# Expert layer one: two successive pairs of experts share one frame of output rows

## The reference, cut to what matters

```python
# layer one of the reference (hier_moe), one expert layer of a two-block decoder
g_prob = softmax(t @ w_group_router + b_group_router)            # 4 groups, the best one
g_w, g_idx = lax.top_k(g_prob, 1)
e_logits = (t @ w_expert_router + b_expert_router).reshape(-1, 4, 8)[group of the token]
e_prob = softmax(e_logits)
e_w, e_idx = lax.top_k(e_prob, 2)                                # 2 of its 8 experts
weights = g_w * e_w / sum(e_w)
combine = one_hot(expert ids) weighted by weights                # (tokens, 32)
a = einsum('nd,edf->nef', t, w_gate)                             # 1024 x 256, 32 experts
b = einsum('nd,edf->nef', t, w_up)
hid = silu(a) * b * combine[:, :, None]
routed = einsum('nef,efd->nd', hid, w_down)                      # 256 x 1024
shared = (silu(t @ w_sh_gate) * (t @ w_sh_up)) @ w_sh_down
out = routed + shared
```

## Time and profile before

| | us |
|---|---|
| median of 3 runs | 982.15 (981.96 to 983.21) |
| the profiled execution | 983.41 |
| its span in the trace | 981.6 |
| TensorE busy | 919.2 (94%) |
| VectorE busy | 306.9 (31%) |
| ScalarE busy | 207.2 (21%) |
| moved by DMA | 339.86 MB, 346 GB/s over the span |

### The profile page before, as it was taken

One profiled execution on the slowest core, in us unless ns is written; L12 is line 12 of the kernel. 1 busy time (PEld: TensorE's weight loads), 2 busy tenths in 40 slices (PEclk: granted clock), 3 DMA queues, 4 the chain that ended last, 5 costly groups with the idle time before them and its releaser, 6 DMA issues.

```text
span 981.6 us, 11709 instructions
## 1 busy us (share of the span) xinstructions
PE 919.2 (94%) x4653; PEld 491.2 (50%) x4653; DVE 306.9 (31%) x664; ACT 207.2 (21%) x440; POOL 23.3 (2%) x60
## 2 busy tenths in 40 slices
PE   8999999999999997999999999999998888798986
PEld 5777566556656555866547353333333333333332
DVE  3346367333333334123317132221111122211213
ACT  4233353122112113123423021111011111101112
POOL 4001300000000000000000000000000000000000
PEclk9999999999999998999999999999999999999998
DMA  9950545999999999754377999999999999999994
GB/s 316 391 181 1 181 184 206 420 420 422 420 421 420 422 420 392 285 171 138 106 299 277 415 385 425 427 425 424 428 428 430 428 429 429 427 427 425 421 421 161
DMA packets 54550, 339.86 MB, mean 346 GB/s; under 512 B 9981, under 2 KB 11025, under 8 KB 24674
## 3 DMA queue, kind: packets, MB, share of 16 engines
q1 hardware_dynamic: 48624, 337.59, 84.7%
q10 hardware_dynamic: 5458, 1.39, 0.6%
q0 software_dynamic: 416, 0.16, 0.1%
HBM read 338.07 MB, written 1.05 MB: 345 GB/s over the span
## 4 chain that ended last, share of the span: by engine, by line
PE 74%; DMA 18%; DVE 5%; ACT 1%; issue 1%; SPq 0%; DVEq 0%; ACTq 0%
PE ps L1227 27%; DMA ring<-in_expert_w_gate_dram 13%; PE ps L1291 10%; PE ps L2359 8%; PE ps L2508 5%; PE ps L1310 5%; PE ps L2575 4%; DMA ring<-in_expert_w_down_dram 3%; DMA ring<-in_w_up_dram 2%; PE ps L2347 1%; PE ps L1133 1%; PE ps L1265 1%; PE ps L2449 1%; PE ps L1459 1%; PE ps L1666 1%
## 5 line engine op out<-in xcount | busy, mean ns | idle before, releaser
L1227 PE MATMUL ps<-ring,work 128*64 128x256 f32 (+1 forms) x2024 | 335.9, 486 | 14.7 <-DMA ring<-in_expert_w_up_dram 8.0
L1227 PEld LDWEIGHTS ps<-ring,work 128*64 128x64 f32 x2024 | 148.7, 137 | 193.3 <-issue 149.8
L1291 PE MATMUL ps<-ring,work 128*64 128x512 f32 x600 | 136.6, 597 | 9.2 <-DMA ring<-in_expert_w_down_dram 6.7
L967 DVE TENSOR_TENSOR work<-work,ps 128x256 f32<-128x256 f32 (+1 forms) x30 | 16.4, 546 | 266.0 <-PE ps L1227 266.0
L2359 PE MATMUL ps<-xT,ring 128*128 128x256 f32 (+1 forms) x384 | 87.0, 385 | 0.0
L1291 PEld LDWEIGHTS ps<-ring,work 128*64 128x64 f32 x600 | 43.7, 137 | 84.3 <-issue 74.0
L1310 PE MATMUL ps<-parts 128*128 128x512 f32 x248 | 73.5, 419 | 6.0 <-DVE parts L1004 6.0
L2359 PEld LDWEIGHTS ps<-xT,ring 128*128 128x128 f32 x384 | 73.2, 193 | 11.6 <-issue 1.2
L1310 PEld LDWEIGHTS ps<-parts 128*128 128x128 f32 x248 | 42.0, 189 | 41.0 <-DVE parts L1004 18.3
L795 ACT ACTIVATE work<-ps,small 128x512 f32<-128x512 f32 x30 | 20.6, 687 | 193.9 <-PE ps L1291 185.8
L789 ACT ACTIVATE work<-ps 128x256 f32<-128x256 f32 (+1 forms) x31 | 15.1, 487 | 208.8 <-PE ps L1265 208.8
(11 more groups left out here) (387 smaller groups left out, 749.4 us busy)
## 6 DMA issues: line engine op xcount, KB each, us to landing
ring<-in_expert_w_gate_dram SPq DMA_DIRECT2D x20, 2048.0 KB, 17.2
ring<-in_expert_w_up_dram SPq DMA_DIRECT2D x20, 2048.0 KB, 17.4
ring<-in_w_gate_dram SPq DMA_DIRECT2D x32, 1024.0 KB, 17.1
ring<-in_w_up_dram SPq DMA_DIRECT2D x32, 1024.0 KB, 18.6
ring<-in_w_down_dram SPq DMA_DIRECT2D x32, 1024.0 KB, 16.0
ring<-in_expert_w_down_dram SPq DMA_DIRECT2D x16, 2048.0 KB, 18.7
ring<-in_expert_w_gate_dram SPq DMA_DIRECT2D x23, 1024.0 KB, 11.2
ring<-in_expert_w_up_dram SPq DMA_DIRECT2D x22, 1024.0 KB, 11.3
```

The lines of the kernel that those rows point to most:

```text
L1227: mm = pe.matmul(ps[CAP * e:CAP * e + CAP, 4 + which, 0:ff], slots, chunks[e][:, k, :], start=(k0 + k == 0), stop=(k0 + k == KC - 1), skip ...
L1291: mm = pe.matmul(ps[CAP * e:CAP * e + CAP, 6 + half, :], hT[:, c0 + k, CAP * e:CAP * e + CAP], columns(chunks[e], k, half), start=(c0 + k ...
```

## The change

Two successive pairs, 2f and 2f + 1, form a frame. Both add their down products into the same PSUM banks 6 and 7 before these are read: the first pair starts the accumulation and the second ends it. For that, the tokens of expert 4f + 2 must stand in rows that expert 4f leaves free, and those of 4f + 3 in rows that 4f + 1 leaves free. So place() shifts slots: from each window start of the second pair it takes off the count of the first (at most 64), and adds this count to the slots of its tokens (share_frames, eight operations for VectorE). A further round is needed now as well when two experts that share rows have more than 64 tokens together, so there may be one round more, and the count of rounds has an operation more, and one for the maximum.

Since rows of both pairs are mixed in the output, the slot's weight can't be applied to it any more; it goes into hidden instead (weighted_hidden). The 0/1 matrices of both pairs are added up (scat_first, scat). ScalarE rounds the output from PSUM (take_frame), VectorE subtracts from PSUM (low_parts), and the scatter follows once per frame, in the next even pair. The transposes of the weighted one-hot now come before hidden is formed: for pair 0 between gates and ups, for the others behind down of the pair before, in the upper half of bank 5. Hidden's transposes go to the upper half of bank 4. The shared products move to pairs 8 and 10.

```diff
-MAX_ROUNDS = TOK // CAP
+MAX_ROUNDS = TOK // CAP + 1
...
+        scat_first = parts[:, 4864:5120].rearrange("p (t s) -> p t s", s=P)
...
-        SHARED_UP, SHARED_DOWN = 7, 11
+        SHARED_UP, SHARED_DOWN = 8, 10
...   # ScalarE
+            def take_frame(n, m):
+                act.wait_ge(ev("y0p"), n + 1)
+                act.activation(y_high[:, 0:512].bitcast(F32R), ps[:, 6, :], ACT.Copy).then_inc(ev("y_parts"), 2)
+                act.wait_ge(ev("y_parts"), n * 4)
+                act.wait_ge(*products_done(cfg, m, per))
+                act.activation(y_high[:, 512:D].bitcast(F32R), ps[:, 7, :], ACT.Copy).then_inc(ev("y_parts"), 2)
...
-                take_down(m, sfx)
+                if tag == "m2" or sfx:
+                    take_down(m, sfx)
+                elif odd:
+                    take_frame(n, m)
...   # VectorE
+            def take_weights(n, odd, bank=5, at=256):
+                turned = ps[:, bank, at:at + 256]
+                dve.wait_ge(ev("scatp"), n + 1)
+                dve.tensor_reduce(slot_weight, turned, AX, ALU.max).then_inc(ev("scat"), 1)
+                turned = turned.rearrange("p (t s) -> p t s", s=P)
+                if odd:
+                    dve.scalar_tensor_tensor(scat.bitcast(F32R), turned, 0.0, scat_first, ALU.is_gt, ALU.add)\
+                        .then_inc(ev("scat"), 1)
+                else:
+                    dve.tensor_scalar(scat_first.bitcast(F32R), turned, 0.0, None, ALU.is_gt).then_inc(ev("scat"), 1)
+                dve.wait_ge(ev("scat"), n * 2 + 2)
+            def weighted_hidden(n, m):
+                dve.wait_ge(ev("sil"), n + 1)
+                dve.wait_ge(*products_done(cfg, m, ups))
+                dve.scalar_tensor_tensor(hs[:, 0:ff], sil[:, 0:ff], slot_weight, ps[:, 5, 0:ff], ALU.mult, ALU.mult)\
+                    .then_inc(ev("h"), 1)
+            def low_parts(n):
+                for half in range(2):
+                    cut = slice(512 * half, 512 * half + 512)
+                    dve.wait_ge(ev("y_parts"), n * 4 + (4 * half - 2))
+                    dve.tensor_tensor(y_low[:, cut].bitcast(F32R), ps[:, 6 + half, :], y_high[:, cut], ALU.subtract)\
+                        .then_inc(ev("y_parts"), 2)
+            def frame(p, first=False):
+                build_weighted(p, p)
+                if first:
+                    take_weights(p, 0, bank=7, at=0)
+                else:
+                    take_weights(p, 0)
+                    low_parts(p - 1)
+                build_weighted(p + 1, p + 1)
+                weighted_hidden(p, p)
+                if isinstance(p, int) and p == SHARED_UP:
+                    take_shared_ups()
+                take_weights(p + 1, 1)
+                weighted_hidden(p + 1, p + 1)
...   # TensorE, down()
-                                               start=(c0 + k == 0), stop=(c0 + k == fc - 1), skip_group_check=True)
+                                               start=(c0 + k == 0 and part != 1),
+                                               stop=(c0 + k == fc - 1 and part != 0), skip_group_check=True)
...
+            def frame(q, q_first, turn, first):
+                for odd in range(2):
+                    p = 2 * q_first + odd
+                    n = q * 2 + odd
+                    alone = p if isinstance(turn, int) else -1
+                    get = getter(p, turn)
+                    def weights_taken():
+                        if first and not odd:
+                            turn_weights(n)
+                        else:
+                            pe.wait_ge(ev("scat"), n * 2 + 2)
+                    if alone == 0:
+                        pe.wait_ge(ev("sh_sil"), TT)
+                    j = gates_and_ups(get, chunk_used, n, odd, first and not odd, pair=alone if alone >= 0 else None,
+                                      between=weights_taken)
+                    if not first and not odd:
+                        scatter(n - 1, 0, alone == 2, False)
+                    if alone == SHARED_UP:
+                        scatter(n - 1, 1, False, False)
+                        shared_ups()
+                    turn_hidden(n, bank=4, at=256)
+                    if not first and not odd and alone != SHARED_UP:
+                        scatter(n - 1, 1, alone == 2, False)
+                    if alone == SHARED_DOWN:
+                        turn_shared()
+                        pe.wait_ge(ev("sh_hT"), 1)
+                        shared_down_products()
+                    if alone == SHARED_UP:
+                        pe.wait_ge(ev("sh_h"), TT)
+                    down(get, chunk_used, j, n, pair=alone if alone >= 0 else None, part=odd)
+                    if alone != PAIRS - 1:
+                        turn_weights(n + 1, bank=5, at=256)
...   # VectorE, place(), before r_c and starts_i are written
+            def share_frames():
+                counts = ps[:, 7, 192:224].rearrange("p (f j) -> p f j", j=4)
+                shared = em[:, 0, 0:16].rearrange("p (f j) -> p f j", j=2)
+                added = em[:, 1, 0:16].rearrange("p (f j) -> p f j", j=2)
+                starts = first_slot[:, 0:EXPERTS].rearrange("p (f j) -> p f j", j=4)[:, :, 2:4]
+                chain(dve.tensor_scalar(shared, counts[:, :, 0:2], float(CAP), None, ALU.min))
+                chain(dve.tensor_tensor(starts, starts, shared, ALU.subtract))
+                chain(dve.tensor_tensor(added, counts[:, :, 2:4], shared, ALU.add))
+                chain(dve.tensor_reduce(r_pair, em[:, 1, 0:16], AX, ALU.max))
+                for tt in range(TT):
+                    mine = routed[:, tt, :].rearrange("p (f j) -> p f j", j=4)[:, :, 2:4]
+                    own = posm[:, tt, :].rearrange("p (f j) -> p f j", j=4)[:, :, 2:4]
+                    chain(dve.tensor_tensor(added, mine, shared, ALU.mult))
+                    chain(dve.tensor_tensor(own, own, added, ALU.add))
...
+            if tag == "m1":
+                chain(dve.tensor_tensor(r_c, r_c, r_pair, ALU.max))
             for k in range(1, MAX_ROUNDS):
```

87 lines of the change are left out of this document (40 added, 47 removed).

## The result

The changed kernel takes 985.2 us (983.56 to 986.97, 12 runs) where the kernel before takes 982.15 (980.62 to 983.21, 12 runs): a ratio of 1.0027, 95% interval 1.0019 to 1.0035. The forecast was 982.8 with a range that ended at 984.8. Rival (c) had the sign too, and the cause is mostly another than its own.

A forecast was written before the change was run, and what follows sets the result against it. The prediction took the DMA weight stream to pace expert layer one, TensorE being quicker. Eight operations +1.7, pair 0's wait +0.3, tail -0.9 and -0.45 sum to +0.65 us: 982.8 from 982.15, range 979.9 to 984.8.

The forecast's parts named there:

- Rival (c): Pair 0's wait for its one-hot passes whole to the DMA stream: up to +2.05 us, 984.2; chance 0.13.
- What bounds the kernel before: Expert layer one: the DMA weight stream paces, 14.9 us a pair of experts; TensorE is quicker at 13.0.
- The eight operations, +1.7: Start of layer one: VectorE's eight chained operations delay TensorE's gather and pair 0, not hidden: +1.7 us.
- Rival (b): Start of layer one: the eight operations slip beside the wait for the gather: -1.35 us, 980.8; chance 0.12.
- Pair 0's wait: Between gates and ups of pair 0, TensorE waits 1.3 us for the weighted one-hot; DMA stream loses +0.3 us.
- the 1.6 us from an issue to first bytes: Weight loads of layer one: about 1.6 us from a load's issue to its first bytes, used for the stream's gaps.
- TensorE would enter pair 15 earlier by 7 x 0.7 less the 3.6 it lost ..., 1.3 us: Last pair of layer one: odd pairs save 0.7 us each, the start loses 3.6; TensorE arrives 1.3 us earlier.
- Even pairs are as before: Even pairs of layer one: TensorE's time unchanged by the change, 0 us.
- The shared products: Layer one: moving the shared products from pairs 7 and 11 to 8 and 10 costs nothing, with or without slack.
- The tail, -0.9 and -0.45: Pair 15: gap from ups to down shrinks from 2.51 to 1.60 us (-0.9); shorter copy and split behind down (-0.45).
- rival (d): Pair 15: waits for weights drop TensorE to half clock, up to +7.3 us, 990; chance 0.07.
- Rival (a): Layer one: TensorE paces after all, or DMA makes up its late start; TensorE alone -2.6 us, 979.5; chance 0.16.

The follow-up runs named there:

- Experiment 6: Kernel before without the seven scatters in odd pairs from pair 3 on, their waits kept: 981.44 us, before 982.33, ratio 0.9984.
- experiment 3: Changed kernel with the eight shift operations replaced by one tiny fill that sets r_pair: 983.76 us, before 982.33, ratio 1.0015.
- experiment 5: Changed kernel without six of its eight scatters (all but first and last), waits kept: 983.71 us, before 982.33, ratio 1.0010.
- experiment 7: Changed kernel with the transposes of the next pair's weights moved from behind down into TensorE's gaps: 983.14 us, before 982.49, ratio 1.0000.
- the mended one: Changed kernel with all repairs, ScalarE taking pair 0's gates before waiting for the moved window starts: 981.69 us, before 982.05, ratio 0.9997.
- 9: Changed kernel with transposes in gaps, pair 0's one-hot built earlier, eight operations behind the first takes: first 982.93 us (ratio 1.0004), then the mended one, 981.69.
- 8: Kernel before, no frames, with layer one's routing-weight transposes moved behind down of their own pair: 989.66 us, before 982.05, ratio 1.0071.

## Why the prediction was wrong

- **What bounds the kernel before:** right. Experiment 6 takes 14 us of work from TensorE and gets 0.6 (profile) to 0.9 us (medians) back.
- **The eight operations, +1.7:** right; 1.77 in the profile of the changed kernel, and by adding or removing them alone the start of pair 0 moves by 1.77 and 1.62 and the end of the layer by 1.52 and 1.27. Rival (b), a hidden start, is ruled out. Its sum of -1.35 also left out the +0.3, though pair 0's wait stays without the eight operations (1.2 us in experiment 3).
- **Pair 0's wait:** its size was right (1.17 for 1.3, loads within 0.2 us of the forecast ones). Its price to the DMA stream, +0.3, was too small: the last ups land 1.1 us later in experiment 5 and 0.5 later in experiment 7, whose first loads stand as in the changed kernel, and 1.15 later in the mended one, whose loads are late by less. Part of it is the 1.6 us from an issue to first bytes, read from stretches of 2 us; in half microseconds the stream is back above 400 GB/s only 2.1 us behind the issue in the changed kernel (8.91 to 11.0, the table in 9). Why the price does not follow the lateness of the loads is open. Rival (c) had this mechanism; in the changed kernel it isn't what set the end, since TensorE came later still.
- **The step that failed is in the tail: "TensorE would enter pair 15 earlier by 7 x 0.7 less the 3.6 it lost ..., 1.3 us".** Counted from the start of pair 0 the forecast had it enter 3.0 us earlier (7 x 0.7 less 1.9), and it entered 3.96 later; with the late start that is 5.7 later where 1.3 earlier was forecast. Of these 7.0 us, 3.1 are the odd pairs, 2.0 the even ones, 1.5 the shared products and 0.4 pair 0 and the last transposes. The terms were mis-sized. An odd pair saves about 0.25, not 0.7: from gates to down it saves 0.7 and not 0.9 (8.81 us, 198.73 to 207.54, for 9.51, 267.67 to 277.18; the wait for hidden is 0.7 in most odd pairs, 0.6 in pair 15), and the transposes behind down cost 0.46 up to the next gates (3.95, 207.54 to 211.49, for 3.49) and not the 0.22 that the earlier trace rows showed for their old place. "Even pairs are as before" is false for the same reason, +0.29 each. So a frame costs 0.04 us where the forecast had it save 0.7, and what pair 0 lost was never made up. Experiments 7 and 8 show the price of the place from both sides.
- **The shared products, "nothing; without that slack, nothing too":** wrong by about 1.5 us, seen in the pitches and waits of the changed kernel alone; no run moved them by themselves, so their share is not shown by an experiment.
- **The slack itself.** In the kernel before TensorE's order had 0.8 us of it, one wait. I read "the stream binds" as if it would still bind after TensorE lost 3.6 us at the start (1.8 of them counted from the start of pair 0, since the stream starts late as well). With so small a margin the question of which of two nearly equal paces binds had to be worked out anew for the changed kernel, pair by pair, and the outcome hung on a price of 0.2 us that was taken from another place of the order.
- **The tail, -0.9 and -0.45:** right (-0.92 and about -0.4). In experiments 5, 7 and 9, whose last ups wait as before, it takes 11.7 to 11.8 us from their start to the end for 12.96, 1.2 to 1.3 less; there it is given back to the later landing.
- **The clock, rival (d):** it did not happen, but the waits of 1 to 2.6 us that it needs did not come either. The granted clock was 1.00 from 200 to 370 us, and 1.00 at 370 to 386. The kernels with waits for weights of up to 1.3 us kept it as well (1.00 at 360 to 380 in 5, 6 and 7). Of the Trainium skill's "TensorE: Matmul & The Clock Gate", section "HAM oscillation — how this bites in real kernels", this shows only that waits of this length did not bring the fall that it describes for a loop with a long wait in every round; no run here had longer ones in this stage. Behind the stage TensorE waits 4.0 us for the norm, and there the clock does fall (0.51 at 388 to 392).
- **Rival (a)** was right that TensorE would pace, wrong in its sum of -2.6 by the same terms (7 x 0.7, the even pairs, the shared products). With the measured ones it is +1.77 + 3.96 - 0.82 - 1.42 = +3.49.

## What to carry to other kernels

Where two streams pace a stage within 1% of each other, neither is "the" bound: work out the new time of both after the change, and take the later one, for each part of the stage. Price an instruction that is moved at its new place, from start to start over its neighbours on both sides; of the 0.70 us that an odd pair saved here, 0.46 were lost to such a move, and over 15 repetitions 0.3 us is 4. Work that is removed is worth its length less what it covered: here 0.9 of 2.06 us in one kind of pair and 0.49 in another.

## What the runs showed of the hardware that I had not expected

- Two transposes of 128x128 cost TensorE 0.22 us between a scatter and down, and 0.52 between down and the next gates (0.37 for themselves, 0.09 on the down ahead, 0.06 on the products behind).
- Eight VectorE operations on 16 elements in a chain of waits step by 0.21 us each, whether they read PSUM or not and whether the view is strided or not.
- The granted clock at 70 to 80 us was 1.00 in seven profiles and 0.83 in the other seven, 1.00, 0.83 and 1.00 in three of the changed kernel; the stage behind layer one took 595.9 to 599.2 us over all of them (598.2 before; 595.9, 596.9 and 598.2 in three of the changed kernel). Two profiles of one kernel (spans 981.7 and 984.9) can so differ by 3 us with the loads of down's chunks in the changed stage equal to 0.02 us. Spans of single executions couldn't have settled this case; lengths from a mark did.
